# A two-layer diffusion step in fp32 on one core: starting matmuls on the high half, an output unit's weights in two parts, and a feed-forward unit's weights split on VectorE

## The chip, the cores and the metric

The kernel runs on one core of one Trainium2 chip. The metric is the device time of one execution in microseconds; lower is better. The kernel before takes 1861.55 us, the median of 3 runs (1857.75 to 1861.74).

## The reference

One inference step of a backbone with two layers, all in fp32, over 640 tokens (128 context tokens and 512 latent tokens) of 1024 features:

```python
# layer 0: differential attention; layer 1: bidirectional mLSTM; each followed by a gated ConvFFN
x <- LN(ALPHA * x + gate * sublayer(x * (1 + scale) + shift))     # post-norm, four times in all
u = dwconv3(h @ w_up, conv_w, conv_b); g, val = split(u)          # ConvFFN: 1024 -> 2 x 2816 -> 1024
ffn = (silu(g) * val) @ w_down
attention: h @ w_qkv, 2D RoPE, softmax(q1 k1) - lam * softmax(q2 k2), times v, RMS norm per head, @ w_o
mLSTM:     h @ w_in (q, k, v, o, gates), conv + silu on q and k, scan over the tokens both ways, norm, @ w_out
```

shift, scale and gate come from a linear map of the conditioning vectors (the "modulation"). Outputs are the tokens, the new attention cache and the new mLSTM states.

## The kernel before

**Layout.** Activations are held transposed: feature on the partition, token on the free axis. `X` is 8 tiles of 128 features by 640 tokens. A *unit* is one 128-column block of a weight matrix; with `KT` = 8 feature tiles it is one 128x1024 load.

**Products.** Every fp32 operand is held as a rounded high half and a remainder in fp32r: `Hh` and `Hl` for activations, `whi` and `wlo` for weights. A product is three terms, high x high, low activation x high weight, high activation x low weight, each in two matmuls of 320 tokens: 6 matmuls for one feature tile, 48 for a unit (`tile`, L571). The result is in one of two PSUM buffers, `pj[0]` and `pj[1]`; successive units of a pair use one each.

**Weights.** SyncE loads a unit into `wraw[k]` (k = unit mod 2) as soon as the low half of the unit before in that buffer has been made (`load`, L354). ScalarE makes `whi[k]` (`split`, L1094) when TensorE is done with the unit that used the buffer; GpSimd subtracts and makes `wlo[k]` (`split_run`, `out_split`), and counts `w_lo`. For the third unit of a feed-forward (the first to use buffer 0 again) there are buffers of their own, `wnh` and `wnl` (L1163, L477), so that they can be made while the first pair still runs.

**Borders.** At each border between stages TensorE has to wait for activations:

- *Layer norm* (`layer_norm`, L1125 and L1683): the last tile's sum and square go to TensorE, VectorE makes the variance, ScalarE makes rstd by Ln and Exp and copies it to PSUM, VectorE multiplies mean by rstd and then, tile by tile, multiplies `X` by rstd and subtracts. `h_build` (ScalarE, L1107) modulates a tile and rounds it (`Hh`, counted in `h_hi`), GpSimd subtracts (`h_lo`, L517: `Hl`, counted in `h_ready`). `h32` has two buffers, so ScalarE can be two tiles ahead of GpSimd.
- *First pair* (`first_pair`, L594): both units of the first pair are done together, tile by tile, each after the wait for its `Hl`. The mLSTM's entry does the same with the gate weights and unit q (L1075).
- *Attention output* (L804, L850 to L867): unit 0 takes the heads' outputs 0 to 5 within the last head; then come the last turn, the last values, the last rms sum, unit 0's steps 6 and 7, unit 1 whole, and `project_rest`. Each step waits for `o_ready`, GpSimd's remainder of that output (`output_lo`, L486).
- *mLSTM output* (L1050 to L1063): the same, but both units take the outputs 0 to 5 early; 6 and 7 come last, for one unit after the other.
- In the output projections VectorE adds each finished unit, gated, to `X` (`gated`, L1655) and counts `pj_added`; a unit waits for the add of the unit before it in its PSUM buffer. ScalarE squares the tile, GpSimd adds the squares.
- *Last norm* (L1585, L556): VectorE normalises the tiles 0 to 4, GpSimd 5 to 7, ScalarE applies the affine map and SyncE stores.

Each engine's order is written out by hand and held by semaphores. There is no planner.

## Time and profile before

| | |
|---|---|
| median of 3 runs | 1861.55 us (1857.75 to 1861.74) |
| the profiled execution | 1860.71 us |
| its span | 1858.9 us |
| mean granted TensorE clock | 0.97 |
| TensorE (PE), matmuls | 1732.8 us busy, 93% |
| VectorE (DVE) | 1047.1 us, 56% |
| ScalarE (ACT) | 696.7 us, 37% |
| GpSimd (POOL) | 646.2 us, 35% |
| chain that ended last | PE 81%, DVE 7%, ACT 4%, issue 2%, DMA 2% |

Busy time is the time in which at least one instruction of the engine runs. The chain is followed back from the last instruction, at each step to what released it; its shares say in which engine the time of the span lies. The granted clock is the share of TensorE's full clock (2.4 GHz) that it was given; its lower level is 0.50 (1.2 GHz). "Issue" is time in which an engine waited for nothing that the profile shows.

### The profile page before, as it was taken

How to read it: one execution, taken by the hardware profiler on the slowest of the kernel's cores; microseconds unless marked ns; L12 is line 12 of the kernel's file. 1: busy time of each engine (PE TensorE's matmuls, PEld its weight loads, DVE VectorE, ACT ScalarE, POOL GpSimd, SP SyncE). 2: the span in 40 equal slices, each digit the busy share in tenths (PEclk: the TensorE clock that was granted, in tenths of full speed). 3: DMA queues.
4: the chain of work that ended last, by engine and by line, in shares of the span. 5: the costliest groups of instructions: out<-in, count | busy, mean ns of one | idle time of the engine just before them, and what ended most of it. 6: DMA issues, size and time to landing. Idle time of an engine off the chain costs nothing.

```text
span 1858.9 us, 29900 instructions
## 1 busy us (share of the span) xinstructions
PE 1732.8 (93%) x11444; PEld 1619.4 (87%) x11444; DVE 1047.1 (56%) x1651; ACT 696.7 (37%) x1074; POOL 646.2 (35%) x292
## 2 busy tenths in 40 slices
PE   6999999777999999999978999997879999999996
PEld 3688888667989999899977999997879999999995
DVE  1377767645766614667337545544558781277833
ACT  3355555534432212323236445644253331133323
POOL 3211221335633332333435232122655333233444
PEclk8999999788999999999999999999989999999998
DMA  9722222002355223453211112110212222222221
GB/s 381 261 63 66 63 69 59 28 25 66 106 191 205 83 74 114 147 204 122 80 63 40 40 52 68 45 54 22 68 46 68 79 82 77 68 68 79 80 79 56
DMA packets 54032, 169.32 MB, mean 91 GB/s; under 512 B 7728, under 2 KB 13232, under 8 KB 53936
## 3 DMA queue, kind: packets, MB, share of 16 engines
q1 hardware_dynamic: 47600, 163.79, 25.6%
q10 hardware_dynamic: 6336, 4.20, 0.7%
q8 instruction: 67, 1.10, 0.2%
q14 instruction: 29, 0.24, 0.0%
HBM read 159.04 MB, written 4.72 MB: 88 GB/s over the span
## 4 chain that ended last, share of the span: by engine, by line
PE 81%; DVE 7%; ACT 4%; issue 2%; DVEq 2%; DMA 2%; POOL 1%; ACTq 0%; SPq 0%; POOLq 0%
PE pj L587 69%; PE mO L967 2%; PE psO L759 2%; DMA awr<-in_w_ada 2%; PE pfrow L608 1%; PE psS L724 1%; DVE pr L1802 1%; PE psT L740 1%; POOL X L538 1%; ACT pr L1217 1%; DVE sm L1787 1%; PE mS L923 1%; PE prow L608 1%; DVE h32t L1823 1%; DVE Al L1813 1%
## 5 line engine op out<-in xcount | busy, mean ns | idle before, releaser
L467 POOL TENSOR_TENSOR wlo<-wraw,whi 128x1024 fp32r<-128x1024 f32 (+1 forms) x130 | 333.4, 2565 | 827.7 <-ACT whi L1099 827.7
L587 PE MATMUL pj<-Hh,whi 128*128 128x320 f32 x2400 | 570.6, 319 | 51.2 <-issue 19.0
L587 PE MATMUL pj<-Hh,wlo 128*128 128x320 f32 x2400 | 553.0, 312 | 0.0
L587 PE MATMUL pj<-Hl,whi 128*128 128x320 f32 x2400 | 552.8, 312 | 0.0
L587 PEld LDWEIGHTS pj<-Hh,whi 128*128 128x128 f32 x2400 | 404.1, 191 | 82.6 <-issue 55.4
L587 PEld LDWEIGHTS pj<-Hl,whi 128*128 128x128 f32 x2400 | 407.6, 191 | 0.0
L587 PEld LDWEIGHTS pj<-Hh,wlo 128*128 128x128 f32 x2400 | 406.8, 190 | 0.0
L1099 ACT CAST whi<-wraw 128x1024 fp32r<-128x1024 f32 (+1 forms) x182 | 201.5, 1108 | 329.8 <-PE pj L587 292.4
L1707 DVE SCALAR_TENSOR_TENSOR fcv<-fus,vec,fcv 128x127 f32<-128x127 f32 (+1 forms) x176 | 229.3, 1344 | 15.2 <-issue 15.2
L1666 DVE SCALAR_TENSOR_TENSOR X<-pj,mods,X 128x128 f32<-128x128 f32 (+1 forms) x144 | 54.5, 434 | 274.7 <-PE pj L587 274.6
L587 PE MATMUL pj<-Gh,whi 128*128 128x320 f32 x704 | 160.5, 309 | 0.0
L587 PE MATMUL pj<-Gh,wlo 128*128 128x320 f32 x704 | 160.5, 309 | 0.0
L587 PE MATMUL pj<-Gl,whi 128*128 128x320 f32 x704 | 160.2, 309 | 0.0
L1104 ACT COPY fus<-pj 128x640 f32<-128x640 f32 x88 | 61.0, 693 | 219.9 <-PE pj L587 219.5
L1710 DVE SCALAR_TENSOR_TENSOR fcv<-fus,vec,fcv 128x127 f32<-128x127 f32 (+1 forms) x176 | 126.2, 758 | 15.6 <-issue 15.6
L499 POOL TENSOR_TENSOR wlo<-wraw,whi 128x1408 fp32r<-128x1408 f32 (+1 forms) x28 | 87.9, 3142 | 110.2 <-ACT whi L1099 110.2
L1704 DVE TENSOR_SCALAR fcv<-fus,vec 128x640 f32<-128x640 f32 x88 | 59.3, 673 | 107.7 <-ACT fus L1104 107.6
L587 PEld LDWEIGHTS pj<-Gl,whi 128*128 128x128 f32 x704 | 117.8, 188 | 0.0
L587 PEld LDWEIGHTS pj<-Gh,whi 128*128 128x128 f32 x704 | 117.8, 188 | 0.0
L587 PEld LDWEIGHTS pj<-Gh,wlo 128*128 128x128 f32 x704 | 117.5, 188 | 0.0
L1175 ACT CAST Gh<-fpr 128x640 f32 (+1 forms) x44 | 32.0, 727 | 215.4 <-DVE fpr L1729 215.4
L530 POOL TENSOR_TENSOR wlo<-wraw,whi 128x1024 fp32r<-128x1024 f32 x24 | 59.7, 2489 | 127.3 <-ACT whi L1099 127.3
(302 smaller groups left out, 2049.4 us busy)
## 6 DMA issues: line engine op xcount, KB each, us to landing
wraw<-in_w_up SPq DMA_DIRECT2D x88, 512.0 KB, 3.3
fwr<-in_w_ada SPq DMA_DIRECT2D x56, 512.0 KB, 5.7
wraw<-in_w_dn SPq DMA_DIRECT2D x32, 704.0 KB, 4.0
awr<-in_w_ada SPq DMA_DIRECT2D x40, 512.0 KB, 10.8
wraw<-in_w_qkv SPq DMA_DIRECT2D x24, 512.0 KB, 3.4
wraw<-in_w_mlin SPq DMA_DIRECT2D x24, 512.0 KB, 3.3
sx<-h32t SPq DMA_DIRECT2D x128, 32.0 KB, 2.0
wraw<-in_w_wo SPq DMA_DIRECT2D x8, 512.0 KB, 3.4
```

Source lines behind the costliest of these rows:

```text
L467: nc.gpsimd.tensor_tensor(wlo[k][:, 0:width], wraw[k][:, 0:width], whi[k][:, 0:width].bitcast(F32), ALU.subtract).then_inc(w_lo, 1)
L499: nc.gpsimd.tensor_tensor(wlo[k][:, 0:width], wraw[k][:, 0:width], whi[k][:, 0:width].bitcast(F32), ALU.subtract).then_inc(w_lo, 1)
L530: nc.gpsimd.tensor_tensor(wlo[v % 2][:, 0:width], wraw[v % 2][:, 0:width], whi[v % 2][:, 0:width].bitcast(F32), ALU.subtract).then_inc(w_l ...
L587: last = mm(out[:, c, 0:HALF], w, x[:, j, c * HALF:(c + 1) * HALF], start=(j == 0 and n == 0), stop=(j == n_k - 1 and n == 2))
L608: last = mm(out[g:g + 32, :], conds[:, 2 * kp + r, PAD - 2 * b:PAD - 2 * b + 32], bufs[u % len(bufs)][:, r, :], start=(b == 0 and kp < 2), ...
L759: last = mm(psO[:, :], v_[par][:, c, :], t_[:, c, :], start=(c == 0 and n == 0), stop=(c == 4 and n == 2))
L1099: nc.scalar.copy(whi[k][:, 0:width], wraw[k][:, 0:width]).then_inc(w_hi, 1)
L1104: nc.scalar.copy(dst.rearrange("p (a b) -> p a b", a=2), pj[k if pairs == 2 else 0][:, :, 0:HALF]).then_inc(pj_copied, 1)
L1666: last = stt(out=x, in0=pj[k][:, bank, c0:c1], scalar=gt, in1=x, op0=ALU.mult, op1=ALU.add)
L1704: ts(c[:, :], f[:, :], tap[1], bias, ALU.mult, ALU.add)
L1707: stt(out=c[:, t0 + 1:t1], in0=f[:, t0:t1 - 1], scalar=tap[0], in1=c[:, t0 + 1:t1], op0=ALU.mult, op1=ALU.add)
L1710: last = stt(out=c[:, t0:t1 - 1], in0=f[:, t0 + 1:t1], scalar=tap[2], in1=c[:, t0:t1 - 1], op0=ALU.mult, op1=ALU.add)
```

## The change

Four edits, with the order of instructions that goes with them:

1. **High half first.** `tile` can do the terms apart. The two terms that need only `Hh` come first, behind a wait for `h_hi`; the third comes behind the wait for `Hl`. The first pairs, the mLSTM's entry (`gates`, q) and the last outputs of both projections do this. At the attention's output, unit 1's steps 0 to 6 and unit 0's step 6 are put between the last turn, the last values and the rms sum; step 5 of unit 0 moves behind turn 3, and ScalarE copies turn 4 before it rounds output 6.
2. **Third output unit in two parts.** Its first `CUT` = 6 tiles (768 columns) are split before the first pair ends, when unit 0 has done its tiles 0 to 5 (`part_used`); the last 256 columns are split when unit 0 is done. On GpSimd the low half of the first part stands ahead of the remainder of output 7 (attention) and of outputs 6 and 7 (mLSTM).
3. **Third feed-forward unit on VectorE**, both halves (`wnh`, `wnl`), ahead of its convolutions.
4. **Norms.** The mean is subtracted first, for `LEAD` = 2 tiles before rstd is there, and the product with rstd comes second. The product of mean and rstd is gone. In the last norm GpSimd subtracts a copy of the mean (`ss`) and then multiplies.

The core of the diff:

```diff
-                        pool.wait_ge(w_hi, base + first + 1)
-                        nc.gpsimd.tensor_tensor(wnl[:, :], wraw[0][:, 0:D], wnh[:, :].bitcast(F32), ALU.subtract).then_inc(w_lo, 1)
+                        pool.wait_ge(w_lo, base + first + 1)
...
-                loop(pool, KT, body)
+                loop(pool, early, body)
+                pool.wait_ge(part_hi, n + 1)
+                nc.gpsimd.tensor_tensor(wlo[0][:, 0:CUT * P], wraw[0][:, 0:CUT * P], whi[0][:, 0:CUT * P].bitcast(F32),
+                                        ALU.subtract).then_inc(part_lo, 1)
+                for j in range(early, KT):
+                    pool.wait_ge(h_hi, KT * h_inst + j + 1)
+                    nc.gpsimd.tensor_tensor(Hl[:, j, :], src[:, j, :], Hh[:, j, :].bitcast(F32), ALU.subtract).then_inc(o_ready, 1)
...
+            def first_pair(pair, ready, base, inst, js=FULL, reads=((), ())):
+                for j in js:
+                    pe.wait_ge(h_hi, KT * inst + j + 1)
+                    for k in range(2):
+                        tile(pair, k, [j], pairs=2, read=reads[k], terms=(0, 1))
                     pe.wait_ge(ready, base + j + 1)
                     for k in range(2):
-                        tile(pair, k, [j], n_k, src, pairs=2, read=reads[k])
+                        tile(pair, k, [j], pairs=2, terms=(2,))
...
+            out_unit(1, [0])
             turn(DA_HEADS - 1, 4)
+            out_unit(1, [1, 2])
             values_lat(DA_HEADS - 1)
+            out_unit(1, [3, 4])
             rms(DA_HEADS - 1)
+            out_unit(0, [6])
+            out_unit(1, [5, 6])
+            def project_rest(base, n, added):
+                v = base // 2 + 1
+                tile(v, 0, range(CUT), pairs=2, read=(pj_added, added + 3), weights=(part_lo, n + 1))
+                tile(v, 0, range(CUT, KT), pairs=2, weights=(w_lo, base + 3))
+                tile(v, 1, FULL, pairs=2, read=(pj_added, added + 4))
...
-            tile(U_WO // 2, 1, FULL, pairs=2, read=(pj_added, 2))
-            project_rest(U_WO, 0)
+            first_pair(U_WO // 2, o_ready, 0, 1, js=(7,))
+            project_rest(U_WO, 0, 0)
...
-                    out(0, range(6, 8))
-                    out(1, range(6, 8))
+                    first_pair(U_MLOUT // 2, o_ready, KT, 4, js=(6, 7))
...
+            def part_split(base, n):
+                act.wait_ge(w_landed[0], 16 * (base // 2 + 2))
+                act.wait_ge(part_used, n + 1)
+                nc.scalar.copy(whi[0][:, 0:CUT * P], wraw[0][:, 0:CUT * P]).then_inc(part_hi, 1)
...
             rms(DA_HEADS - 1)
+            part_split(U_WO, 0)
             output_hi(O32, onorm, (KT - 1,))
...
-                dve.wait_ge(rstd_ready, n + 1)
-                tt(st_mu[:, :, 0:HALF], st_mu[:, :, 0:HALF], rs[:, :, :], ALU.mult)
-                dve.wait_ge(rstd_psum, n + 1)
-                for j in range(KT if n < 3 else SIDE[0]):
-                    x = X[:, j, :].rearrange("p (a b) -> p a b", a=2)
-                    tt(x, x, st_va[:, :, 0:HALF], ALU.mult)
-                    dve.drain()
-                    tt(x, x, st_mu[:, :, 0:HALF], ALU.subtract).then_inc(xn_ready, 1)
+                tiles = KT if n < 3 else SIDE[0]
+                for j in range(tiles + LEAD):
+                    if j == LEAD:
+                        dve.wait_ge(rstd_psum, n + 1)
+                    if j >= LEAD:
+                        x = X[:, j - LEAD, :].rearrange("p (a b) -> p a b", a=2)
+                        tt(x, x, st_va[:, :, 0:HALF], ALU.mult).then_inc(xn_ready, 1)
+                    if j < tiles:
+                        x = X[:, j, :].rearrange("p (a b) -> p a b", a=2)
+                        tt(x, x, st_mu[:, :, 0:HALF], ALU.subtract)
+                    if j > 0:
+                        dve.drain()
...
             def ffn(layer, base):
+                for k in range(2):
+                    dve.wait_ge(w_landed[k], 16 * (base // 2 + 2))
+                ts(wnh[:, :], wraw[0][:, 0:D], 1.0, None, ALU.mult).then_inc(w_hi, 1)
+                dve.drain()
+                tt(wnl[:, :], wraw[0][:, 0:D], wnh[:, :].bitcast(F32), ALU.subtract).then_inc(w_lo, 1)
```

## Rows read from the trace of the kernel before

**Rows 1.** The page's busy line: busy us (share of the span) xinstructions.

```profile
PE 1732.8 (93%) x11444; PEld 1619.4 (87%) x11444; DVE 1047.1 (56%) x1651; ACT 696.7 (37%) x1074; POOL 646.2 (35%) x292
```

**Rows 2.** Chain of waits, an earlier head, then the attention's output: start us, us, what.

```profile
158.25 3.43 PE psO L759 x15
...
380.91 6.54 PE psO L759 x15
...
387.47 0.59 ACT O L1278
...
391.86 0.90 DVE O L1848
...
392.78 0.73 ACT Hh L1274
...
393.71 1.54 POOL Hl L491
```

**Rows 3.** Windows there: us, busy us (x) PE, PEld, DVE, ACT, POOL; PEclk, DMA, GB/s.

```profile
372.96:376.38 3.42, 1.47 (x6) 0.68 (x4) 2.30 (x6) 2.53 (x6) 0.00 (x0) 1.00 0.00 0
376.38:379.79 3.41, 1.33 (x5) 0.93 (x5) 1.93 (x3) 2.38 (x4) 0.19 (x1) 0.56 0.01 2
386.62:390.03 3.41, 1.92 (x8) 1.20 (x6) 0.00 (x0) 1.32 (x2) 0.00 (x0) 0.94 0.00 0
390.03:393.44 3.41, 1.11 (x7) 0.77 (x5) 1.43 (x7) 2.11 (x3) 0.00 (x0) 1.00 0.00 0
```

**Rows 4.** Chain of waits at the mLSTM's output projection.

```profile
1291.42 3.53 PE pj L587 x24
...
1302.04 0.73 ACT Hh L1274
...
1304.55 3.58 PE pj L587 x12
...
1308.24 1.06 ACT whi L1099
...
1309.36 2.37 POOL wlo L499
```

**Rows 5.** Timeline, first layer norm: start us, us, instruction, [idle before <-releaser].

```profile
456.41 0.82 DVE L1698 TENSOR_TENSOR X<-X,st_va 128x640 f32<-128x640 f32 x1
457.31 0.82 DVE L1700 TENSOR_TENSOR X<-X,st_mu 128x640 f32<-128x640 f32 x1
...
458.16 1.20 ACT L1114 ACTIVATE h32t<-X,lb,la 128x128 f32<-128x128 f32 x2 [1.78 <-DVE X L1700]
...
459.42 0.72 ACT L1116 CAST Hh<-h32t 128x640 fp32r<-128x640 f32 x1
...
473.76 1.58 POOL L521 TENSOR_TENSOR Hl<-h32t,Hh 128x640 fp32r<-128x640 f32 x1 [0.60 <-ACT Hh L1116]
...
475.29 2.41 POOL L477 TENSOR_TENSOR wnl<-wraw,wnh 128x1024 fp32r<-128x1024 f32 x1
```

**Rows 6.** Chain of waits at the third layer norm.

```profile
1358.67 9.27 issue
1367.93 16.81 PE pj L587 x96
```

**Rows 7.** Timeline, VectorE at the mLSTM's output projection.

```profile
1308.16 1.14 DVE L1666 SCALAR_TENSOR_TENSOR X<-pj,mods,X 128x128 f32<-128x128 f32 x3 [4.50 <-PE pj L587]
...
1309.39 3.02 DVE L1680 TENSOR_TENSOR sx<-sx,X 128x640 f32<-128x640 f32 x1
```

**Rows 8.** Timeline, last layer norm.

```profile
1842.68 0.49 DVE L1690 TENSOR_SCALAR sx<-sx 128x640 f32<-128x640 f32 x1
...
1844.83 1.54 POOL L559 TENSOR_TENSOR X<-X,rs 128x640 f32<-128x640 f32 x1 [13.46 <-ACT rs L1132]
...
1852.87 3.35 ACT L1590 ACTIVATE X<-X,xb,xa 128x640 f32<-128x640 f32 x4 [0.70 <-DVE X L1700]
1852.89 1.54 POOL L563 TENSOR_TENSOR X<-X,sx 128x640 f32<-128x640 f32 x1
```

More of the change, by code:

```diff
@@ L497, in out_split @@
                     k = i % 2
+                    c0 = CUT * P if i == first == 2 else 0
                     pool.wait_ge(w_hi, base + i + 1)
[L499 to L500 removed]
+                    nc.gpsimd.tensor_tensor(wlo[k][:, c0:width], wraw[k][:, c0:width],
+                                            whi[k][:, c0:width].bitcast(F32), ALU.subtract).then_inc(w_lo, 1)
                     if i >= 3:
@@ L569, in _, with tile @@
             mm = nc.tensor.matmul
-            def tile(pair, k, ks, n_k=KT, src=None, pairs=1, read=None, spare=None):
+            def tile(pair, k, ks, n_k=KT, src=None, pairs=1, read=None, spare=None, terms=(0, 1, 2), weights=None):
                 v = 2 * pair + k
@@ L576, in tile @@
                 out = pj[k if pairs == 2 else 0]
-                if ks[0] == 0:
+                if weights:
+                    pe.wait_ge(*weights)
+                elif ks[0] == 0 and terms[0] == 0:
                     pe.wait_ge(w_lo, v + 1)
+                if ks[0] == 0 and terms[0] == 0:
                     if read is None and (not isinstance(v, int) or v > 0):
@@ L786, in wo @@
                         pe.wait_ge(o_ready, j + 1)
-                        tile(U_WO // 2, 0, [j], pairs=2)
+                        done = tile(U_WO // 2, 0, [j], pairs=2)
+                    return done
                 scores(h, 0)
@@ L826, in head @@
                 turn(h, 3)
+                if last:
+                    wo([5]).then_inc(part_used, 1)
                 if nxt2:
@@ L877, in m_wait, with unit, gates @@
                     pe.wait_ge(mt_free, MUSE[use])
-            def unit(what, h, ks):
+            def unit(what, h, ks, terms=(0, 1, 2)):
                 v = U_MLIN + _ml_unit(what, h)
-                tile(v // 2, v % 2, ks, read=(pj_copied, MCOP + _ml_unit(what, h)))
-            def gates(j):
-                for n, (x, w) in enumerate(((Hh, wgh), (Hl, wgh), (Hh, wgl))):
+                tile(v // 2, v % 2, ks, read=(pj_copied, MCOP + _ml_unit(what, h)), terms=terms)
+            def gates(j, terms):
+                for n in terms:
+                    x, w = ((Hh, wgh), (Hh, wgl), (Hl, wgh))[n]
                     for c in range(2):
@@ L1001, in out @@
                         pe.wait_ge(o_ready, KT + j + 1)
-                        tile(U_MLOUT // 2, k, [j], pairs=2, read=(pj_copied, MCOP + 6 * ML_HEADS))
+                        done = tile(U_MLOUT // 2, k, [j], pairs=2, read=(pj_copied, MCOP + 6 * ML_HEADS))
+                    return done
                 def early(w, ks):
```

81 lines of the change are left out of this document (44 added, 37 removed).

## The prediction

> **What bounds the kernel now.** I read the busy line first: TensorE (PE) is at 93% of a span of 1858.9 us [rows 1], so only the rest, and TensorE's own low clock, can be had. Then I followed the chain of waits to find where PE is not the chain, and read the timeline in those stretches. They are seven borders: the first projection (start), the attention's output projection, the four layer norms and the mLSTM's output projection.
>
> At the attention's output projection PE waits for one head's way through ScalarE (ACT), VectorE (DVE) and GpSimd (POOL): values end at 387.45, the copy starts at 387.47, the last normalise at 391.86, its rounded copy Hh at 392.78, the remainder Hl at 393.71, and PE goes on at 395.29 [rows 2]. Its value matmuls there took 6.54 us; the same fifteen took 3.43 us in an earlier head [rows 2]. In the windows the granted clock is 1.00, then 0.56 after PE was busy 1.47 of 3.42 us; after a stretch in which PE was busy 1.92 us it is still 1.00 [rows 3]. At the mLSTM output PE waits for Hl, and again for the low half of the third unit's weights (1309.36 plus 2.37) [rows 4]. At a layer norm PE waits for the steps of [rows 5], from the statistics to the first Hl: 9.27 us in the third [rows 6].
>
> **Prices.** A projection matmul is 0.147 us at the high clock (24 in 3.53) and 0.27 at the low (12 in 3.58, less 0.35 for the last one's latency) [rows 4]. A "step" below is 6 matmuls: 0.88 or 1.6 us.
>
> **Part 1, output projection of the attention.** Unit 1's seven steps for outputs 0 to 6 and unit 0's step 6 move ahead of the last output. One step goes before the last turn, two between turn and values, two between values and the rms sum, three (one of them unit 0's) after it. ACT copies the last turn before it rounds output 6, which takes 0.72 us (the same cast, [rows 2]) off the values' start: 380.91 becomes 380.2, or 380.3 with PE's two steps ended.
> Clock: wo's step 5 moved behind turn 3 adds 0.88 us of work to the stretch that had 1.47, so 2.3 us; that is farther from the row with 0.56 behind it than the 1.92 with 1.00 behind it [rows 3]. So I take the high clock: values 380.3 to V = 383.7. At the low clock the two steps last to 382.1 and the values end near V = 386.0.
> From V: copy and square 1.45, but PE is in its two steps until V+1.76, so the rms sum comes 0.3 late. Normalise before: V+4.4 (387.45 to 391.86) [rows 2]; now V+4.7, Hh at V+5.6 to V+6.35. ACT's 768-column piece (part_split) lies beside the normalise: 0.75 of 1.06 us [rows 4] is 0.8, the normalise is 0.9. PE's three steps end at V+5.5: hidden. At V+6.35 PE does the eight matmuls that need no Hl (1.17). POOL first does the low half of the piece, 0.75 of 2.37 = 1.8 us [rows 4], from V+5.6 to V+7.4, and only then Hl, 1.54 [rows 2], to V+9.0: here the change costs 1.0 us against an Hl straight after Hh. Four matmuls follow; unit 0 ends at V+9.5. New wait: unit 2 writes the PSUM buffer of unit 0, whose gated add takes 1.14 us [rows 7] and used to lie beside unit 1. Behind that wait everything on PE is queued, and nothing else waits for PE. Unit 2 starts at V+10.8 = 394.5.
> Before, from 395.29 there were 6+48 matmuls to go to unit 2: nineteen at the low clock, the rest at the high, until about 405.5. From 394.5 I charge 1.3 us for a new spell of low clock (PE is idle for 1.5 us and again for 1.2). Unit 3's weights come at V+17, needed 7 us after 394.5: the ACT and POOL order hides it. SP's load of unit 4 waits for the low half of unit 2 (done about V+11) and has 14 us; hidden. Gain 405.5 - 394.5 - 1.3 = 9.7; at the low clock 7.4. Bounds 5 and 11.5.
>
> **Part 2, layer norms 1 and 3.** The mean is subtracted from two tiles while ACT does Ln and Exp; the multiplication of mean by rstd goes. rstd still has to be copied to PSUM, which ended beside it, so the first product stays at 456.41 and the subtract behind it, 0.82 and its drain, leaves the path: 0.9 us [rows 5]. PE now starts on Hh, not on Hl: 1.54 of POOL and 0.1, so 1.65 us. Start 2.55 us earlier. The end of the first pair is set by two things. Hl of tile 7 ended at 475.34 (473.76 plus 1.58), now 0.9 earlier, plus four matmuls, 0.6: 475.0. PE from 459.3 with 96 matmuls, 14.1 us, and 2.1 for the low clock: 475.5. The third unit's weights were split by ACT and POOL after Hl, POOL's part 475.29 plus 2.41 [rows 5], so PE began unit 2 at 477.8. On DVE they are made at about 468 to 472, behind its last product; ahead of PE by 3 us. What they cost: no row shows the 1024-column copy or subtract on DVE; from below the 128x640 products, 0.82 each [rows 5], from above POOL's own 2.41. I take 0.6 and 1.1, as DVE is freed only from POOL's lock. POOL's Hl operations, 1.58 each, come every 1.9 us there (ACT's 1.20 and 0.72 for a tile) and must let them in: one Hl is late by 0.3, one by 1.1, at the end 0.5 is left: 475.5. Behind them on DVE wait the convolutions, which need a finished unit of the first pair, so they are not late. Unit 2 at 475.7: gain 2.1, bounds 1.0 and 3.5. In the third norm PE's own pace was the limit (96 in 16.81 us, from 1367.93) [rows 6]; 2.55 earlier, and a shorter low spell or not: 2.8, bounds 1.0 and 4.0.
>
> **Part 3, layer norm 2 (mLSTM entry).** Same edit without the third unit; 96 matmuls again, and its Hl cadence allows 0.9 plus 1.2 at the end. A start well ahead of the rise of the clock wins least: I take 1.0, bounds 0.5 and 2.5. The gate chain behind it moves with it.
>
> **Part 4, mLSTM output.** Start on Hh at 1302.8 instead of 1304.55 [rows 4]. 24 matmuls: 3.5 us high, 6.4 low; 5.8 as it begins low. Unit 0 ends 0.3 before them, then 0.45 of latency and 1.14 of add [rows 7]: unit 2 at 1309.9 against 1311.85. But POOL's 1.8 us piece, ready 0.8 us after ACT's rstd, falls on DVE's four final multiplications, which are on the path and end at 1302.04, where ACT's cast begins [rows 4]. The row for such a meeting: the sum into sx, two SBUF inputs of 128x640, took 3.02 us from 1309.39 [rows 7] beside POOL's split from 1309.36 to 1311.73 [rows 4]; a product of that size takes 0.82 [rows 5]. So one of DVE's operations waits until POOL ends: up to 1.8 us, I take 1.2. Gain 0.8, bounds -0.7 and 3.
> The Trainium skill (SBUF — State Buffer, "SBUF: two separate sides") calls this an exclusive lock of the port pair, taken by a DVE operation with two SBUF inputs or in a 2-port mode against a GpSimd one; by that rule, the trace agrees with its 3.02 us. Without the rule, port shared in proportion, Part 4 would gain about 1.4.
>
> **Part 5, last norm.** POOL's first operation waited for rstd until 1844.83; it now subtracts the mean copy that DVE makes behind 1842.68 plus 0.49 (estimated at 0.7, less than a product), so from 1844.0. Its last product, before at 1852.89 plus 1.54, ends near 1853.6; DVE's last tile comes some 2.4 earlier, as two multiplications of 0.82 and one subtract leave its path. ACT's last tile ended at 1852.87 plus 3.35 [rows 8], now near 1854.6. Gain 1.6, bounds 0.8 and 2.2.
>
> **Part 6, start.** PE begins on Hh 0.9 us early, at the low clock, and later waits for the modulation weights: 0.3, bounds 0 and 0.9.
>
> **Sum.** 9.7 + 2.1 + 2.8 + 1.0 + 0.8 + 1.6 + 0.3 = 18.3 us. The profiled execution took 1860.71 with its span of 1858.9: 1842.4. The median of the three runs, 1861.55, lies 0.84 higher: 1843.2.
>
> **Rivals.**
> (a) The low clock stays at the output projection: the steps put into PE's gaps run at 0.27 and the values at 6.54. For it: the row with 0.56 [rows 3]. Against: the gaps are filled. Gain there 7.4, or 5 with a second slow spell: 14 to 16 in all, 1846.5.
> (b) POOL is the new bound: its lock and its order (the piece ahead of the last Hl) at the two output projections and at DVE's weights. Then Part 4 is -0.7, Parts 2 lose 1 each, Part 1 loses 1.5: 18.3 - 5 = 13.3, so 1848.2. For it: 3.02 against 0.82 us. Against: DVE's normalise is over when POOL starts in Part 1.
> (c) Clock windfall: the first pairs rise early and the projection has no second slow spell: +4.5, 1838.7.
> (d) Slower. PE now stops twice in each tile of a first pair, for Hh and for Hl, and for this the clock does not rise in the four first pairs and the matmuls behind them. If 96 matmuls in four places and the 48 behind them stay at the low clock, that costs 0.12 each: 576 x 0.12 = 69, less 8 us that the low spells cost now, less the 18.3 gained: 1861.55 + 43 = 1904. It decides from 150 more slow matmuls on (18.3 / 0.12). Against: at the low clock a tile takes PE 3.2 us and a new one comes every 1.9, so PE never stops there.
> (e) The weights' order doesn't do what it says: a unit's weights still come last. Then Part 1 loses the add's overlap and more, about 4: 1847.
>
> **Chances.** Forecast 0.48, (a) 0.17, (b) 0.16, (c) 0.09, (e) 0.06, (d) 0.04. Range: 1837.5 takes in (c), 1851 takes in (a), (b) and (e) with Part 1 at 5. A measurement of this kernel tells a change from none at about 0.2%, 3.7 us: faster means under 1857.8. All but (d) and a piece of (b) are there: faster 0.94, same 0.02, slower 0.04.
>
> **What would show it.** Right: the fifteen value matmuls of the last head near 3.4 us; unit 2 of the attention's output within 11 us of the values' end, its wait put down to DVE's add; PE's idle in norms 1 and 3 near 6.7 us in place of 9.3; no wait for the low half of a third unit; in the mLSTM output one of DVE's final products over 1.5 us. Wrong: low clock over 380 to 390; DVE's copy or subtract of the weights above 3 us; PE waiting for Hl in each tile; the end of ACT less than 1 us nearer the last statistics.

## The result, and the profile after

The changed kernel takes 1841.11 us, the median of 5 runs (1838.96 to 1844.45), against 1858.02 us for the kernel before on the same chip (5 runs, 1854.0 to 1861.74). The ratio is 0.9907, 95% interval 0.9892 to 0.9921: 0.9% faster. The profiled execution took 1841.11 us, its span 1839.3 us; between the two profiled spans lie 19.6 us, between the two medians 16.9. Every run is in the fast state but one of the kernel before, beside e1 to e4, which took 6382.6 us and is in no ratio.

The page's busy line of the changed kernel, against [rows 1]: the same number of matmuls in 7 us less of TensorE's busy time. Units are counted from 0 here: unit 2 is the third unit of its stage, the first to use a weight buffer again.

```profile
PE 1725.6 (94%) x11444; PEld 1613.5 (88%) x11444; DVE 1050.2 (57%) x1651; ACT 694.4 (38%) x1074; POOL 642.7 (35%) x292
```

The chain of waits of the changed kernel at the attention's output and the first norm, its longest pieces (start us, us, what). It answers to [rows 2] and [rows 5].

```profile
381.10 3.56 PE psO L777 x15
384.65 1.75 PE pj L601 x12
389.98 1.74 DVEq L1693
391.79 1.43 DVE la L1692
395.99 43.82 PE pj L601 x288
444.12 6.92 issue
451.04 16.73 PE pj L601 x94
```

The fifteen value matmuls are at the high clock (3.56 in place of 6.54). The wait for ScalarE, VectorE and GpSimd is still there, but two small operations of VectorE stand in it, which the prediction did not name. The norm's idle time is 6.92 in place of 9.44.

The timeline there, in the changed kernel (start us, us, instruction, idle before it <- what ended it):

```profile
389.86 1.82 POOL L498 TENSOR_TENSOR wlo<-wraw,whi 128x768 fp32r<-128x768 f32 x1 [7.41 <-ACT whi L1175]
389.89 1.82 DVE L1690 TENSOR_SCALAR xa<-vec 128x8 f32<-128x8 f32 x1
...
391.64 1.54 POOL L502 TENSOR_TENSOR Hl<-O,Hh 128x640 fp32r<-128x640 f32 x1
391.70 1.52 DVE L1692 TENSOR_SCALAR la<-mods 128x16 f32<-128x16 f32 x1
...
394.71 1.14 DVE L1711 SCALAR_TENSOR_TENSOR X<-pj,mods,X 128x128 f32<-128x128 f32 x3
...
395.99 0.87 PE L601 MATMUL pj<-Hh,whi 128*128 128x320 f32 x2 [1.90 <-DVE X L1711]
```

These are the coefficients of norm 1. `xa` (8 columns) and `la` (16 columns) each start just behind an operation of GpSimd and end with it; `xb`, between the two, takes 0.16. Where GpSimd is idle beside them, as in e1 and e10, `xa` and `la` take 0.17 us too. Unit 0 was done at about 393.85, its gated add came at 394.71.

The timeline of the changed kernel at the mLSTM's output, against [rows 4] and [rows 7]: VectorE's two final products meet GpSimd's piece, and unit 2 waits for the add, not for weights.

```profile
1283.88 3.24 DVE L2151 SCALAR_TENSOR_TENSOR hO<-hO,vec,rs 128x640 f32<-128x640 f32 x2 [5.67 <-ACT rs L1514]
1284.64 1.80 POOL L498 TENSOR_TENSOR wlo<-wraw,whi 128x768 fp32r<-128x768 f32 x1 [21.01 <-ACT whi L1175]
...
1296.05 0.53 PE L601 MATMUL pj<-Hh,whi 128*128 128x320 f32 x2 [1.02 <-DVE X L1711]
```

The timeline of the changed kernel at norm 1, against [rows 5]. VectorE makes the third unit's weights from 459.76, GpSimd's last two remainders take 3.80 together, and TensorE waits for neither: before unit 2 it waits for ScalarE's copy of unit 0 out of PSUM.

```profile
459.76 0.95 DVE L1765 TENSOR_SCALAR wnh<-wraw 128x1024 fp32r<-128x1024 f32 x1 [0.16 <-issue]
...
460.80 2.42 DVE L1767 TENSOR_TENSOR wnl<-wraw,wnh 128x1024 fp32r<-128x1024 f32 x1
...
462.38 3.80 POOL L532 TENSOR_TENSOR Hl<-h32t,Hh 128x640 fp32r<-128x640 f32 x2 [0.23 <-ACT Hh L1151]
...
468.68 0.53 PE L601 MATMUL pj<-Hh,wnh 128*128 128x320 f32 x2 [0.64 <-ACT fus L1139]
```

In the kernel before there is no wait at that place. Its chain of waits there has the first pair and the 96 matmuls of units 2 and 3 in one piece:

```profile
461.87 30.27 PE pj L587 x192
```

The timeline puts the first matmul of unit 2 at 477.83, straight behind the pair; the low half of its weights had been ready at 477.70 [rows 5].

**Where the time went, by stage.** Lengths in us between landmarks that every kernel has: the value matmuls of heads 6 and 7, the variance of each norm, the first gate matmul, ScalarE's last square in the mLSTM, the end. The columns are the start up to the first landmark, last head, attention output, norm 1 with its feed-forward, entry of the mLSTM, its four heads, its output, norm 3 with its feed-forward, last norm.

```
                 start  head7  attout  norm1  entry  mlstm  mlout  norm3   last
before          345.48  35.43   71.73 515.41   9.28 316.36  65.01 483.08  17.13
changed         346.48  34.50   63.35 514.15   6.75 313.65  63.99 480.95  15.52
e1 att undone   346.49  35.19   71.62 514.20   6.76 314.02  63.84 480.90  15.52
e2 mlout undone 344.82  34.53   64.65 513.42   6.76 315.89  65.01 480.63  15.52
e3 hi-first     346.49  34.52   63.37 514.47   8.38 315.31  63.90 481.22  15.52
e4 norm order   345.54  34.64   63.41 514.65   7.65 315.87  63.91 481.70  17.10
e5 ffn weights  346.19  34.41   63.38 514.19   6.76 313.60  63.97 481.58  15.52
e6 coefficients 345.70  34.23   61.24 513.44   6.76 316.07  63.76 480.85  15.52
e7 last tile    348.88  34.58   63.38 513.59   6.76 318.22  63.14 480.51  15.51
e8 remainders   345.21  34.11   62.00 513.44   6.75 315.25  62.85 481.21  15.52
e9 step 5       345.25  34.66   64.66 513.46   6.76 315.91  63.96 480.96  15.52
e10 no parts    344.61  34.51   65.30 513.45   6.76 316.14  67.97 480.64  15.52
e11 combined    346.50  34.54   60.40 513.25   6.76 313.95  62.31 480.41  15.51
e12 e11,weights 346.50  34.41   60.41 513.69   6.75 313.57  62.44 481.43  15.51
```

From the first two rows: -1.00 + 0.93 + 8.38 + 1.26 + 2.53 + 2.71 + 1.02 + 2.13 + 1.61 = 19.57 us. Read down a column among kernels that share the stage's code, and it shows what an execution alone does: the start 344.6 to 348.9, the mLSTM's heads 313.6 to 318.2, the attention's output 62.0 to 64.7, norm 1 513.4 to 514.2, norm 3 480.6 to 481.2; but the entry 6.75 to 6.76, the mLSTM's output 63.8 to 64.0, the last norm 15.51 to 15.52. A difference counts where it is outside these.

Two of the spreads can be narrowed. In the norms it lies in the first pair, that is, in when TensorE's clock rises there: its 96 matmuls in norm 1 took 17.01 us in the changed kernel (e1 17.05, e5 16.99) and 16.29 or 16.30 in e2, e6, e8, e9 and e10, all with the same code and the same start, 6.71 us behind the variance. From the first matmul of unit 2 to the next landmark, norm 1 takes 489.8 us (490.2 before, 489.9 in e5) and norm 3 takes 457.0 in every kernel, before included, but 457.6 in e5 and 457.2 in e12. And the column "entry" ends at the first gate matmul, so it shows when TensorE starts there and not what stays of it. VectorE's first operation behind that first pair comes 25.95 us behind the variance in the kernel before, 24.09 in the changed one, and 24.0 to 25.1 over the ten other executions with its code there.

### The profile page after: what moved, and what is told of

The parts are those of the page before. It is cut to its first block, busy times and chain, and to the rows that moved or that the text cites. A ratio compares the mean times of both kernels' runs of the same rounds, so it can differ in the third digit from the quotient of the medians.

```text
span 1839.3 us, 29894 instructions
## 1 busy us (share of the span) xinstructions
PE 1725.6 (94%) x11444; PEld 1613.5 (88%) x11444; DVE 1050.2 (57%) x1651; ACT 694.4 (38%) x1074; POOL 642.7 (35%) x292
## 4 chain that ended last, share of the span: by engine, by line
PE 82%; DVE 7%; ACT 4%; DVEq 2%; issue 2%; DMA 2%; POOL 1%; ACTq 0%; SPq 0%; POOLq 0%
PE pj L601 69%; PE mO L999 2%; DMA awr<-in_w_ada 2%; PE psO L777 2%; PE psS L742 1%; PE pfrow L626 1%; PE psT L758 1%; DVE pr L1856 1%; ACT pr L1260 1%; POOL X L549 1%; DVE sm L1841 1%; PE mS L955 1%; PE prow L626 1%; DVE h32t L1877 1%; PE mT L1024 1%
## 5 line engine op out<-in xcount | busy, mean ns | idle before, releaser
L601 PE MATMUL pj<-Hl,whi 128*128 128x320 f32 x2400 | 546.3, 311 | 1.0 <-POOL Hl L502 1.0
L510 POOL TENSOR_TENSOR wlo<-wraw,whi 128x1408 fp32r<-128x1408 f32 (+2 forms) x28 | 83.9, 2995 | 105.5 <-ACT whi L1134 101.7
```

The costliest lines, as they stand in the source:

```text
L510: nc.gpsimd.tensor_tensor(wlo[k][:, c0:width], wraw[k][:, c0:width], whi[k][:, c0:width].bitcast(F32), ALU.subtract).then_inc(w_lo, 1)
L601: last = mm(out[:, c, 0:HALF], w, x[:, j, c * HALF:(c + 1) * HALF], start=(j == 0 and n == 0), stop=(j == n_k - 1 and n == 2))
```

## The experiments

Each of e1 to e10 is the changed kernel with one edit; e12 is e11 with one edit. Ratios are to the kernel before on the same chip, as 0.9907 is. By the intervals of the ratios only e1, e4 and e10 (slower) and e11 (faster) stand apart from the changed kernel; the others have to be read from the stages. V is the end of the last head's value matmuls.

### e1: the attention's output as before

```diff
-                if last:
-                    wo([5]).then_inc(part_used, 1)
...
-            out_unit(1, [0])
             turn(DA_HEADS - 1, 4)
-            out_unit(1, [1, 2])
             values_lat(DA_HEADS - 1)
-            out_unit(1, [3, 4])
             rms(DA_HEADS - 1)
-            out_unit(0, [6])
-            out_unit(1, [5, 6])
...
-            part_split(U_WO, 0)
```

> The changed kernel with the attention's output projection alone as before (order of TensorE's steps, third unit's weights split whole, ScalarE's order). Theory A, the parts add up and this one is worth what the two traces show between 364.5 us and the end of the first norm's statistics, 8.8 us: 1841.1 + 8.8 = 1849.9 us, the value matmuls of the last head at 6.5 us again in place of 3.56, statistics' end 8.8 us later, and the later borders as in the changed kernel. Theory B, the change there was worth more than that because the later stages met TensorE's low clock at another phase (the mLSTM's first head gained 3.1 us by it): 1852 to 1854, with the mLSTM's first head slow again. Theory C, the steps only moved time (given back later): under 1846.

Measured 1850.33 us, ratio 0.9951 (0.9937 to 0.9965). Theory A: the stage is 8.3 us longer, with the last head 9.0, and every later stage is within 0.4 of the changed kernel's. The windows of that kernel and of the changed one (us, busy us and count of PE, granted clock, DMA, GB/s), first e1:

```profile
376.00:381.00 5.00, 2.27 (x9) 0.63 0.00 2
381.00:390.00 9.00, 6.82 (x17) 0.63 0.00 0
```

```profile
376.00:381.00 5.00, 4.63 (x28) 1.00 0.01 2
381.00:390.00 9.00, 9.00 (x50) 1.00 0.01 2
```

### e2: the mLSTM's output as before

```diff
-                    first_pair(U_MLOUT // 2, o_ready, KT, 4, js=(6, 7))
+                    out(0, range(6, 8))
+                    out(1, range(6, 8))
...
-            part_split(U_MLOUT, 1)
```

> The changed kernel with the mLSTM's output projection alone as before. Theory A, that part is worth 1.0 us by the positions of the traces: 1842.1 us; VectorE's first final product takes 1.68 us again in place of 3.24, since GpSimd's piece of weights no longer falls beside it, and unit 2 waits for the low half of the third unit again. Theory B, the lock costs more there than the earlier start brings: 1840 or less.

Measured 1842.24 us, ratio 0.9903 (0.9888 to 0.9919), no difference that medians can tell. By the stage: 65.01, the length before to the hundredth, against 63.99. Theory A, 1.0 us; unit 2 waits for GpSimd's `wlo` again, 1.93 us.

### e3: whole tiles behind Hl in the first pairs

```diff
-                    pe.wait_ge(h_hi, KT * inst + j + 1)
-                    for k in range(2):
-                        tile(pair, k, [j], pairs=2, read=reads[k], terms=(0, 1))
+                    if js is not FULL:
+                        pe.wait_ge(h_hi, KT * inst + j + 1)
+                        for k in range(2):
+                            tile(pair, k, [j], pairs=2, read=reads[k], terms=(0, 1))
                     pe.wait_ge(ready, base + j + 1)
                     for k in range(2):
-                        tile(pair, k, [j], pairs=2, terms=(2,))
+                        if js is FULL:
+                            tile(pair, k, [j], pairs=2, read=reads[k])
+                        else:
+                            tile(pair, k, [j], pairs=2, terms=(2,))
```

> The changed kernel with whole tiles behind Hl in the first pairs of the start, of norms 1 and 3 and in the mLSTM's entry (the output projections stay as changed). Theory A, TensorE starts 1.65 us later in each norm and ends tile 7 with twelve matmuls in place of four behind the last Hl (1.2 us): +1.2 to +1.65 at each of norms 1, 2, 3, +0 to 0.9 at the start, so 1845 to 1847. Theory B, TensorE's two stops in each tile cost clock or issue (the slower side of the prediction): undoing it brings 1841 or less. Theory C, the pair's end is set elsewhere (ScalarE's copy of the first product, the third unit's weights), so the late start is made up by tile 7: 1842 to 1843.

Measured 1844.31 us, ratio 0.9918 (0.9904 to 0.9932). TensorE starts 1.6 us later in each norm (8.38 against 6.75 at the mLSTM's entry). In norm 1 0.3 us of it stays, in norm 3 0.3, which the stage cannot tell from none, at the start nothing (346.49 against 346.48). At the entry VectorE's first operation behind the pair comes at 25.82 against 24.09, 1.7 us, or 0.7 against the slowest execution of the changed code (25.1). Theory C in the norms, between C and A at the entry; 2.0 in all by the ratios, whose intervals overlap. The windows of norm 1, first e3, then the changed kernel:

```profile
451.00:454.41 3.41, 1.70 (x6) 0.50 0.00 0
454.41:457.82 3.41, 3.41 (x16) 0.61 0.02 5
```

```profile
450.95:454.36 3.41, 3.32 (x12) 0.50 0.03 5
454.36:457.77 3.41, 3.41 (x17) 0.61 0.00 0
```

The clock rises at the same time in both. The earlier start adds six matmuls at the low clock, so 1.65 us of it are worth 0.9 between these two executions, and 0.64 us of that goes into the wait for ScalarE's copy, which e3 does not have (its unit 2 starts without a wait). Against the five executions with a pair of 16.3 us it is worth more: unit 2 starts 24.66 us behind the variance in e3, 24.35 in the changed kernel and 23.64 in those, so 0.3 to 1.0 us. The first pair and units 2 and 3 in the chains of e3 and of e2, which has the changed code here:

```profile
452.71 16.28 PE pj L601 x96
...
469.04 28.47 PE pj L601 x192
```

```profile
450.70 16.01 PE pj L603 x94
...
467.63 28.45 PE pj L603 x192
```

### e4: the norms' arithmetic as before

```diff
+                dve.wait_ge(rstd_ready, n + 1)
+                tt(st_mu[:, :, 0:HALF], st_mu[:, :, 0:HALF], rs[:, :, :], ALU.mult)
+                dve.wait_ge(rstd_psum, n + 1)
...
+                    tt(x, x, st_va[:, :, 0:HALF], ALU.mult)
+                    dve.drain()
+                    tt(x, x, st_mu[:, :, 0:HALF], ALU.subtract).then_inc(xn_ready, 1)
```

> The changed kernel with the norms' arithmetic as before (mean times rstd, product first, subtract second; GpSimd waits for rstd in the last norm). Theory A: +0.9 us at each of norms 1, 2 and 3 and +1.6 at the last: 1841.1 + 4.3 = 1845.4. Theory B, in norms 1 to 3 the pair's end is set by something else than the first tile's date: only the last norm's 1.6, so 1842.7. Theory C, the earlier first product was worth more than its 0.9 because all later tiles' cadence hangs on it: 1847.

Measured 1847.74 us, ratio 0.9938 (0.9924 to 0.9952). By stage +0.5, +0.9, +0.75 and +1.6: 3.7 us, theory A less what the low clock takes in norm 1. (The 0.9 is the start of the entry; VectorE's first operation behind its pair comes 1.8 us later than in the changed kernel, 0.8 later than in the slowest execution of its code.) The profiled span is 5.2 longer, the ratios differ by 5.8 us; the 1.5 to 2 above 3.7 are of the size by which the mLSTM's heads differ between executions (here 315.87).

### e5: the third feed-forward unit's weights on ScalarE and GpSimd

```diff
-                ts(wnh[:, :], wraw[0][:, 0:D], 1.0, None, ALU.mult).then_inc(w_hi, 1)
-                dve.drain()
-                tt(wnl[:, :], wraw[0][:, 0:D], wnh[:, :].bitcast(F32), ALU.subtract).then_inc(w_lo, 1)
...
+                        nc.gpsimd.tensor_tensor(wnl[:, :], wraw[0][:, 0:D], wnh[:, :].bitcast(F32), ALU.subtract).then_inc(w_lo, 1)
...
+                            nc.scalar.copy(wnh[:, :], wraw[0][:, 0:D]).then_inc(w_hi, 1)
```

> The changed kernel with the third feed-forward unit's weights split on ScalarE and GpSimd again. Theory A, the split on VectorE is what lets the third unit start when the pair ends: without it TensorE waits for the low half, GpSimd's 2.4 us behind its last Hl (466.18 in the changed kernel), until about 468.6 to 469.3, against 468.68 now behind ScalarE's copy of unit 0; so 0 to 0.6 us at norm 1 and the same at norm 3: 1841 to 1842.3. Theory B, GpSimd's last Hl come earlier without the lock of VectorE's subtract (two took 3.80 us together in place of 3.15), and undoing it gains: 1840.5. Theory C, the split on VectorE carries most of what the norms gained (2 us each): 1845.

Measured 1843.18 us, ratio 0.9906 (0.9891 to 0.9921). Nothing in norm 1, 0.6 us in norm 3. The size is theory A's, but it does not lie before unit 2, where the waits are as long as in the changed kernel (0.64 and 0.66): it lies before unit 4, the next to use buffer 0, for which GpSimd is late. Timeline of TensorE in that kernel, unit 2 of norms 1 and 3, then unit 4 of norm 3:

```profile
468.25 0.53 PE L602 MATMUL pj<-Hh,wnh 128*128 128x320 f32 x2 [0.58 <-ACT fus L1140]
...
1366.46 0.53 PE L602 MATMUL pj<-Hh,wnh 128*128 128x320 f32 x2 [0.64 <-POOL wnl L482]
...
1381.27 0.55 PE L602 MATMUL pj<-Hh,whi 128*128 128x320 f32 x2 [0.50 <-POOL wlo L542]
```

### e6: the coefficients ahead of the last normalise

```diff
-                if acc:
+                if acc and base != U_WO:
...
+            coefficients((0, 0), mod(0, 3), mod(0, 4))
+            nc.vector.memset(sx[:, :], 0.0)
+            dve.drain()
             normalise(DA_HEADS - 1)
-            coefficients((0, 0), mod(0, 3), mod(0, 4))
```

> The changed kernel with VectorE's coefficients for norm 1 and the zeroing of sx ahead of the last head's normalise. Theory A, two of these small operations waited 1.74 and 1.43 us for GpSimd and so the gated add of unit 0 came 0.9 us late (394.71 against the end of unit 0 near 393.85): unit 2 starts 0.9 us earlier, V + 10.4 after the end of the values in place of V + 11.3, 1840.2. Theory B, moved ahead they stand on the path to the last normalise (VectorE waits there for ScalarE, but has 0.5 us of them left): 0 or a loss of up to 0.5 us. Theory C, unit 0's add comes when TensorE lets it, not later: no change at all.

Measured 1839.64 us, ratio 0.9885 (0.987 to 0.99), 4 us under the changed kernel's by the ratios, whose intervals overlap. Theory A by the places: values end at 383.64, unit 2 starts at 394.18, V + 10.5 in place of V + 11.3, and the add follows unit 0 at once. The rest of the stage's 2.1 us is the clock behind it: 288 matmuls in 42.47 us in place of 43.82. That is no merit of the edit: with the changed kernel's code there the 288 took 42.47 in e8, 43.82 in the changed kernel and 45.10 in e2. `la` took 1.55 us here too, beside GpSimd's remainder of output 6, but nobody waited for it. The timeline of e6:

```profile
392.89 1.14 DVE L1711 SCALAR_TENSOR_TENSOR X<-pj,mods,X 128x128 f32<-128x128 f32 x3 [3.93 <-PE pj L601]
...
394.18 0.53 PE L601 MATMUL pj<-Hh,whi 128*128 128x320 f32 x2 [1.10 <-DVE X L1711]
```

### e7: unit 0 first in a pair's last tile

```diff
+                    if j == LAST:
+                        tile(pair, 0, [j], pairs=2, terms=(0, 1))
+                        pe.wait_ge(ready, base + j + 1)
+                        tile(pair, 0, [j], pairs=2, terms=(2,))
+                        tile(pair, 1, [j], pairs=2)
+                        continue
```

> The changed kernel with another order in the last tile of each first pair: unit 0's six matmuls first, then unit 1's six. Theory A, TensorE is the bound at the pair's end and waits 0.64 and 0.66 us for ScalarE's copy of unit 0 before unit 2 in norms 1 and 3; unit 1's 0.88 us now hide it, and in the mLSTM's output unit 0 and its add come 0.6 us earlier: 1841.1 - 0.64 - 0.66 - 0.6 = 1839.2, the waits gone. Theory B, GpSimd's last Hl is late and sets the end, so eight matmuls instead of four stand behind it: no gain or up to 0.3 us lost at each norm.

Measured 1844.96 us, ratio 0.9903 (0.9889 to 0.9917). Theory A by the places: the mLSTM's output takes 63.14 us, 0.85 less, and in norms 1 and 3 the waits are gone (the 96 matmuls and the 192 follow each other); there the stages' 0.6 and 0.4 us are within what executions do. Yet the profiled span is 5.3 longer: 2.4 from the start and 4.6 from the mLSTM's heads, where this edit changes nothing. The chain of waits of e7 there; the same 24 matmuls take 3.73 us in the changed kernel and 6.22 before.

```profile
453.55 17.03 PE pj L601 x96
470.63 28.45 PE pj L601 x192
...
1014.19 6.08 PE pj L601 x24
```

### e8: remainders 6 and 7 of the mLSTM ahead of the piece

```diff
+LATER = (1,)
...
+                if n not in LATER:
+                    part()
                 for j in range(early, KT):
...
+                if n in LATER:
+                    part()
```

`part()` is the wait for `part_hi` and the subtraction of the 768 columns, which stood where the first call is; 1 is the mLSTM's output.

> The changed kernel with GpSimd making the remainders of outputs 6 and 7 of the mLSTM first and the low half of the third unit's first piece behind them. Theory A (the lock): VectorE's two first final products take 1.68 us in place of 3.24, outputs 6 and 7 are rounded 1.6 us earlier, and the piece, done by about 1291.5 on the changed kernel's scale, is still ahead of unit 2: gain 1.0 to 1.6 us, 1839.5 to 1840.1. Theory B: the products' 3.24 us have another cause (ScalarE's piece beside them) and stay: 0 to 0.3 us. Theory C: the piece becomes what unit 2 waits for, and the gain is given back: unit 2's wait is put down to GpSimd's low half.

Measured 1840.86 us, ratio 0.9893 (0.9877 to 0.9908). Theory A: the stage is 62.85 in place of 63.99, 1.1 us. The timeline of e8, beside that of the changed kernel above:

```profile
1281.76 1.68 DVE L2157 SCALAR_TENSOR_TENSOR hO<-hO,vec,rs 128x640 f32<-128x640 f32 x2 [5.68 <-ACT rs L1520]
...
1288.92 1.83 POOL L500 TENSOR_TENSOR wlo<-wraw,whi 128x768 fp32r<-128x768 f32 x1
...
1292.79 0.53 PE L607 MATMUL pj<-Hh,whi 128*128 128x320 f32 x2 [1.03 <-DVE X L1717]
```

The piece is ready 2 us ahead of unit 2. ScalarE's piece still lies beside the products, so theory B falls: what stretched them is GpSimd's subtraction, the lock that Part 4 priced. It took 1.56 us (3.24 less 1.68), and the new order brings 1.1 of these back.

### e9: unit 0's step 5 back ahead of the last scores

```diff
-                    wo([4])
+                    wo([4, 5]).then_inc(part_used, 1)
...
-                if last:
-                    wo([5]).then_inc(part_used, 1)
```

> The changed kernel with unit 0's step 5 ahead of the last head's scores again instead of behind turn 3. In the changed kernel the last scores ran at TensorE's low clock (2.46 us in place of 1.35 to 1.5) and the value matmuls at the high one. Theory A (the prediction's): the step is what fills the stretch before the values; without it the granted clock falls near 376 to 380 again and the values take 5 to 6.5 us: unit 2 comes 1.5 to 3 us later, 1842.6 to 1844. Theory B: unit 1's three steps about turn 4 are enough to hold the clock; the scores are fast again (0.9 us earlier) and the values stay at 3.5: 1840.2. Theory C: which stretch is slow differs between executions and not with this step: the same time within 1 us.

Measured 1842.32 us, ratio 0.9908 (0.9894 to 0.9921): theory C for the time, and theory B for the values' clock, which stays high without the step. (The last scores are fast here, but so they are in e2, e5, e6, e8, e11 and e12 with the step moved; they take 2.46 us in the changed kernel, e3, e4, e7 and e10.) The last head takes 34.66 us against 34.50, the value matmuls stay at the high clock; the attention's output is 64.66, which e2 has too, with the step moved (64.65); in both the 288 matmuls took 45.1 us. The windows of e9:

```profile
376.00:381.00 5.00, 4.45 (x29) 1.00 0.01 2
381.00:390.00 9.00, 8.34 (x48) 1.00 0.01 2
```

### e10: the third output unit's weights whole

```diff
-            part_split(U_WO, 0)
...
-            acc_tiles(U_WO, 0, D, D, parted=True)
+            acc_tiles(U_WO, 0, D, D)
```

(the same in the mLSTM, and GpSimd's piece with it)

> The changed kernel with the third output unit's weights split whole, in both projections, behind the end of unit 0 (the order of TensorE's steps stays as changed). Attention: GpSimd makes the last remainder 1.8 us sooner, unit 0 ends near V + 8.3, then ScalarE 1.06 and GpSimd 2.4: unit 2 at V + 11.9 in place of V + 11.3. mLSTM: no piece beside VectorE's final products (1.68 in place of 3.24), unit 0 ends 1.6 us sooner, then 1.06 and 2.4 in place of the add's 1.14: unit 2 0.7 us later. Theory A: so the two parts are worth only 1.3 us together, 1842.4, and most of the attention's 9 us is the order. Theory B: the two parts carry more, since unit 3's weights are pushed back too: 1844 to 1846. Theory C: nothing or a gain, GpSimd's piece costs what it brings: 1841 or less.

Measured 1847.0 us, ratio 0.9938 (0.9925 to 0.9952): theory B's size. The waits are those of theory A: unit 2 at V + 12.1 in the attention, and in the mLSTM 14.3 us behind the start of ScalarE's Exp in place of 12.9. These make 0.7 and 1.4 us; the ratios differ by 5.8. The wait in the mLSTM costs more than itself. Timeline and chain of waits of e10:

```profile
1299.31 0.90 PE L598 MATMUL pj<-Hh,whi 128*128 128x320 f32 x2 [3.42 <-POOL wlo L507]
```

```profile
1296.83 2.36 POOL wlo L507
1299.31 45.09 PE pj L598 x288
```

The first two matmuls of unit 2 take 0.90, not 0.53, and the 288 behind the wait 45.09 in place of 42.47 (42.51 in the kernel before): 2.6 us of low clock behind 3.4 us of idle. The granted clock there is 0.50:

```profile
1299.00:1302.00 3.00, 2.69 (x10) 0.50 0.54 157
```

So the stage is 4.0 us longer, 1.4 of wait and 2.6 of clock. It is one profiled execution; that the ratios differ by 5.8 us, and the two output stages by 5.9, says that it was no exception. In the attention's output, where the 288 take 42.5 to 45.1 anyhow, e10 has 45.05, and the cause cannot be told there.

### e11: e6, e7 and e8 together, the remainder first in the attention too

```diff
+LATER = (0, 1)
```

The rest of the edit is that of e6, e7 and e8.

> The changed kernel with three of the edits tried: VectorE's coefficients early, GpSimd's remainders ahead of the piece (in both projections), and unit 0 first in the last tile of each first pair. Theory A, they add: attention 0.8 for the add and 0.9 to 1.6 for the last remainder, mLSTM output 1.1 plus 0.85, norms 0.56 plus 0.46: 4.7 to 5.4 us less than the changed kernel, 1836 median. Theory B, in the attention's output the piece, now behind the last remainder, is what unit 2 waits for, and the clock takes its share: 2.5 to 3.5 us, 1838.

Measured 1834.98 us, ratio 0.9868 (0.9853 to 0.9883), the fastest kernel of this study: its interval and the changed kernel's do not meet. 0.4% under the changed kernel, 7 us by the ratios. By stage: attention 60.40 against 63.35, norm 1 513.25 against 514.15, mLSTM's output 62.31 against 63.99, norm 3 480.41 against 480.95: 6.1 us, of which 1.3 in the attention are the clock (42.48 for the 288). The 4.8 left are theory A's 4.7 to 5.4. The chain of waits of e11; unit 2 starts at V + 9.7.

```profile
381.15 3.58 PE psO L789 x15
...
390.89 1.56 POOL Hl L506
394.44 42.48 PE pj L607 x288
```

### e12: e11 with the third feed-forward unit's weights as before

```diff
-                ts(wnh[:, :], wraw[0][:, 0:D], 1.0, None, ALU.mult).then_inc(w_hi, 1)
-                dve.drain()
-                tt(wnl[:, :], wraw[0][:, 0:D], wnh[:, :].bitcast(F32), ALU.subtract).then_inc(w_lo, 1)
```

This is e5's edit, made on e11.

> The combined kernel with the third feed-forward unit's weights split on ScalarE and GpSimd again, which in the changed kernel alone made no difference (the wait for ScalarE's copy of unit 0 hid it). In the combined kernel that wait is gone. Theory A: now GpSimd's low half, ready about 0.6 to 0.8 us after the pair's end, is what unit 2 waits for in norms 1 and 3: 0.6 to 0.8 us each, 1836.3, and a wait put down to GpSimd's wnl at both places. Theory B: GpSimd's last remainders come earlier without VectorE's subtract beside them and give it back (in norm 3 the combined kernel waits 0.40 us for one of them): 1835 to 1835.5.

Measured 1836.35 us, ratio 0.9878 (0.9862 to 0.9895). Theory A by the places: waits of 0.42 and 0.90 us for GpSimd's low half before unit 2, where e11 has none. The stages are 0.4 us longer in norm 1 (within what executions do) and 1.0 in norm 3, against 0.0 and 0.6 in e5; medians cannot tell e12 from e11. The timeline of e12:

```profile
465.23 0.57 PE L608 MATMUL pj<-Hh,wnh 128*128 128x320 f32 x2 [0.42 <-POOL wnl L483]
...
1362.03 0.56 PE L608 MATMUL pj<-Hh,wnh 128*128 128x320 f32 x2 [0.90 <-POOL wnl L483]
```

## Why the prediction was right

The total, 1843.2 for 1841.1, was right, and each part came within its bounds, the start at their edge. Not all for the reasons given. The gain tells more than the total, since the median of before on which the forecast stood, 1861.55, lies 3.5 above that of the five runs: forecast 18.3, measured 16.9. Part by part the profiles give 9.3 + 3.4 + 1.9 + 1.0 + 1.6 = 17.2, with Part 3 between 0.9 and 1.9 from one execution to the next.

**Part 1 (forecast 9.7; stage and last head 9.3, e1 9.0).** Value matmuls 3.4 forecast, 3.56 measured. Unit 2 forecast at V + 10.8, measured V + 11.3, a little beyond the 11 that was to be the sign; its wait is for VectorE's add, as forecast. Two errors lie under the good sum. *The step that failed:* "wo's step 5 moved behind turn 3 adds 0.88 us of work to the stretch", and so holds the clock. e9 puts it back, and the clock stays: what is left of the edit there, the three steps of unit 1 about the last turn, does it, with PE busy 4.45 of 5.00 us (ScalarE's new order goes with them, and no run took it out alone). In all twelve executions with these steps the value matmuls run at the high clock; in the two without (before, e1) they take 6.5. I had worked out the clock from a step before the gap and not from what fills the gap. *The step left out:* VectorE's coefficients, which I took to be nothing, meet GpSimd's piece; e6 gives back 0.8 us. Of the 1.0 us that I priced for the piece ahead of Hl, 0.8 came back in e11, at V + 9.7. The charge for a second slow spell, 1.3, measured 1.35 (43.82 less 42.47) in the changed kernel; over executions of the same code it is 0, 1.35 or 2.6.
The order of TensorE's steps brings most of the part: without the two parts of the weights 7.3 us of it are still there (e10). The two parts bring 0.7 by the start of unit 2.

**Part 2 (norm 1 forecast 2.1, measured 1.3; norm 3 forecast 2.8, measured 2.1).** The start came 2.52 and 2.5 us earlier, as worked out (2.55). *The step that failed:* "so PE began unit 2 at 477.8". I read the low half of the third unit's weights, ready at 477.70, as what held unit 2. But TensorE ended the first pair only at 477.83 and went on without a wait: its own pace was the limit in norm 1 as in norm 3. So the split on VectorE had no wait to remove before unit 2; it could only keep a new one from showing once the rest came earlier (nothing in e5, 0.42 us in e12). *The terms mis-sized:* the pair and what comes behind it. I had 16.2 us for the 96 matmuls; they took 17.01 in the changed kernel and 16.3 in five other executions of its code, and 15.97 before. Then comes a wait that I did not have, 0.64 and 0.66 us for ScalarE's copy of unit 0. Before, unit 1's last six matmuls lay beside that copy; with the high half first unit 0 ends only two matmuls ahead of unit 1, and the copy lies bare. e3 and e7 show it: where unit 0 ends six matmuls ahead, the wait is gone. In all, unit 2 starts 0.8 us earlier in norm 1 (1.55 in those five) and 2.1 in norm 3; 0.4 us more come later in norm 1. The weights on VectorE were worth 0 and 0.6 in the changed kernel, the 0.6 at unit 4, and 0.4 and 1.0 once e7's wait was gone (e12); the price of their making was 0.95 and 2.42 for my 0.6 and 1.1, and TensorE did not wait for them.

**Part 3 (1.0 forecast).** The first gate matmul is 2.5 us earlier (9.28 to 6.75). At VectorE's first operation behind the pair 1.86 us of it are left in the changed kernel's profile, 0.85 to 1.9 over the eleven executions with its code there: 0.85 to 1.0 in four of them, so that my cut for the low clock holds there, and 1.8 to 1.9 in five.

**Part 4 (0.8 forecast, 1.0 measured in two ways, 65.01 to 63.99 and e2).** The lock took 1.56 us for my 1.2; e8 shows it. The split in two saves more here than I gave it: without it the wait for weights brings 2.6 us of low clock with it (e10).

**Part 5 (1.6 forecast, 1.61 measured).** e4 shows it alone (1.58).

**Part 6 (0.3 forecast).** Nothing: the start with the old order (e3) is 346.49, with the new 346.48, and executions of one code differ by 4.3 us there.

**Rivals.** (a) falls, the clock is 1.00 from 376 to 390. (b) is half right: GpSimd's lock and order cost 0.8, 0.8 and 1.1 us, which e11 recovers; most of it was in the sum already. (c) did not come; the 2.7 us of the mLSTM's heads in the profiled execution are within what executions do, and so chance. (d): TensorE does not stop in the pairs, and the clock rises where it rose. (e) falls: unit 2 waits for VectorE's add and not for weights, and e10 shows what waiting for them costs.

**Medians and traces.** The profiled spans differ by 19.6 us, the medians by 16.9. The mLSTM's heads give 2.7 of the 19.6, and in fourteen profiled executions this stage took 313.6 to 318.2, while none of e1 to e12 changes the heads ahead of their last outputs. The profiled execution of before, 1860.71, was itself 2.7 us above its median of 1858.02. What makes the clock fall there in one execution and not in the next was not isolated. The Trainium skill (TensorE: Matmul & The Clock Gate, "What's actually happening") says that one kernel shows different counts of slow matmuls from run to run; the runs here agree, with 3.73, 5.3 and 6.1 us for the same 24 matmuls (changed kernel, e2, e7).

## What to carry to other kernels

Fill the gap itself: work put between two waits of TensorE held its clock, and one wait of 3.4 us cost 2.6 us more in slow matmuls behind it. Before you price a wait, look whether TensorE stands idle at it: here weights that came 0.13 us ahead of the pair's end looked like the limit and were not. When a wait is removed, look for what used to lie beside it (a copy out of PSUM, an add, tiny coefficient work): it is the next wait, and an edit can be worth nothing until that one is gone. Read an edit's worth from the stage it touches, against the same stage in kernels that share its code; a profiled span alone carries a few us of chance.

## What the runs showed of the hardware

- An operation of VectorE on 8 or 16 columns can take 1.5 to 1.8 us: `xa` and `la`, 0.17 us alone, ended with GpSimd's subtraction beside them (both in the changed kernel and e9, `la` in e6). The Trainium skill (SBUF — State Buffer, "SBUF: two separate sides") says that the first to start has the shared pair for the whole instruction; the traces agree, since `xa` and `la` start 0.03 and 0.06 us behind GpSimd's operation, and operations of 8 and 16 columns were held as one of 640 was.
- Behind 3.4 us of idle at the mLSTM's output TensorE ran at 1.2 GHz for a while, which cost 2.6 us (e10, 45.09 against 42.47, granted clock 0.50); behind 0.3 to 1.9 us of idle there it did not in any other kernel (42.5 in all). In the attention's output 1.9 us of idle cost 0, 1.35 or 2.6 us from one execution to the next.
- When the clock rises at a border differs between executions of the same code: the 96 matmuls of norm 1's first pair, started 6.71 us behind the variance, took 17.0 us in three executions and 16.3 in five. So a start 1.65 us earlier at the low clock was worth 0.3 us or 1.0 at unit 2 (e3 against these).
